# First block of the gated delta rule: the causal mask applied ahead of the exponential, and one raw buffer for z

## What is computed

```python
gcum = jnp.cumsum(g, axis=-1)
diff = gcum[..., :, None] - gcum[..., None, :]
decay = jnp.where(causal, jnp.exp(jnp.where(causal, diff, 0.0)), 0.0)
Lm = jnp.where(strict, jnp.einsum('nbhid,nbhjd->nbhij', kb, k) * decay, 0.0)   # kb = k * beta
T = lax.linalg.triangular_solve(Lm + eye, ...)                                  # inverse of Lm + eye
aqk = jnp.einsum('nbhid,nbhjd->nbhij', q, k) * decay
```

## Time and profile before

| what | value |
|---|---|
| three runs | 1980.54, 1978.75, 1978.02 us; median 1978.75 us |
| the profiled execution | 1971.89 us, its span 1970.1 us |
| mean granted clock of TensorE | 0.964 |
| first delta-rule block, from SyncE's first load to ScalarE's last output | 294.58 to 384.65 us |
| TensorE busy over the whole span | 93% |

### The profile page before, as it was taken

How to read it: one execution, slowest core, us unless ns; L and a number is a source line. 1 busy time by engine, 2 the same in 40 slices (tenths; PEclk the granted TensorE clock), 3 DMA queues, 4 the chain that set the end, 5 groups by cost and what they waited for, 6 DMA issues and landing times. The chain is left out here.

```text
span 1970.1 us, 24088 instructions
## 1 busy us (share of the span) xinstructions
PE 1833.9 (93%) x8588; PEld 1521.2 (77%) x8588; DVE 1496.0 (76%) x1118; ACT 1108.3 (56%) x891; POOL 366.4 (19%) x317
## 2 busy tenths in 40 slices
PE   6999997897999974999999999999999999999991
PEld 5888876796888873788888888888888888888870
DVE  4336567566232645899999999999999999999976
ACT  4123443243331214777777777777777777777751
POOL 0000006142000010322222213222222121221320
PEclk9999997898999986999999999999999999999995
DMA  4322225103233254799999999999999999999955
GB/s 152 107 86 86 85 86 179 29 8 122 93 130 105 73 190 172 313 382 391 366 392 380 379 393 369 386 391 370 389 376 380 395 365 390 395 365 392 377 223 233
DMA packets 124396, 516.93 MB, mean 262 GB/s; under 512 B 20772, under 2 KB 20964, under 8 KB 90244
## 3 DMA queue, kind: packets, MB, share of 16 engines
q1 hardware_dynamic: 114996, 482.30, 63.9%
q0 software_dynamic: 9360, 34.08, 4.3%
HBM read 492.19 MB, written 24.15 MB: 262 GB/s over the span
## 5 line engine op out<-in xcount | busy, mean ns | idle before, releaser
L1609 DVE TENSOR_TENSOR mlo<-mraw,mhi 128x2048 fp32r<-128x2048 f32 x384 | 908.3, 2399 | 62.3 <-ACT mhi L1605 58.4
L1605 ACT ACTIVATE mhi<-mraw 128x2048 fp32r<-128x2048 f32 x384 | 722.7, 1913 | 114.2 <-PE PM L1982 114.2
L1979 PE MATMUL PM<-mhi,xgT_hi 128*128 128x512 f32 x1024 | 404.4, 395 | 0.0
L1980 PE MATMUL PM<-mlo,xgT_hi 128*128 128x512 f32 x1024 | 401.1, 392 | 0.0
L1982 PE MATMUL PM<-mhi,xgT_lo 128*128 128x512 f32 x1024 | 276.4, 392 | 0.0
L1980 PEld LDWEIGHTS PM<-mlo,xgT_hi 128*128 128x128 f32 x1024 | 192.9, 188 | 41.7
L1982 PEld LDWEIGHTS PM<-mhi,xgT_lo 128*128 128x128 f32 x1024 | 192.3, 188 | 42.2
L1979 PEld LDWEIGHTS PM<-mhi,xgT_hi 128*128 128x128 f32 x1024 | 192.8, 188 | 41.0
L1998 PE MATMUL PM<-mhi,hT_hi 128*128 128x512 f32 x512 | 203.9, 398 | 2.6 <-DVE hT_lo L1928 2.6
L1999 PE MATMUL PM<-mlo,hT_hi 128*128 128x512 f32 x512 | 200.5, 392 | 0.0
L1817 POOL TENSOR_TENSOR glu<-glu 128x1024 f32<-128x1024 f32 x32 | 77.2, 2411 | 576.9 <-DVE glu L1923 576.9
(11 more groups left out here) (313 smaller groups left out, 2566.4 us busy)
## 6 DMA issues: line engine op xcount, KB each, us to landing
mraw<-in_w_gate_up_dram SPq DMA_DIRECT2D x256, 1024.0 KB, 8.4
mraw<-in_w_down_dram SPq DMA_DIRECT2D x128, 1024.0 KB, 9.3
raw<-in_w_in_dram SPq DMA_DIRECT2D x24, 1024.0 KB, 5.1
qkvT<-in_w_in_dram SPq DMA_DIRECT2D x8, 1024.0 KB, 5.7
mraw<-expert_rows_scratch SPq DMA_DIRECT2D x8, 1024.0 KB, 10.8
zraw<-in_w_in_dram SPq DMA_DIRECT2D x4, 1024.0 KB, 6.1
qkvT<-in_w_o_gdn_dram SPq DMA_DIRECT2D x4, 1024.0 KB, 5.0
qkvT<-in_w_o_sconv_dram SPq DMA_DIRECT2D x4, 1024.0 KB, 5.1
```

Source lines behind the costliest of these rows:

```text
L1605: nc.scalar.activation(mhi[:, split_slot(m), :], mraw[:, raw_slot(m), :], ACT.Copy).then_inc(e_h, 1)
L1609: nc.vector.tensor_tensor(mlo[:, split_slot(m), :], mraw[:, raw_slot(m), :], mhi[:, split_slot(m), :].bitcast(F32), ALU.subtract).then_inc ...
L1979: pe.matmul(gate_up_bank[:, n, :], xgT_hi[:, k, :], w_hi[:, n, :], start=False, stop=False)
L1980: pe.matmul(gate_up_bank[:, n, :], xgT_hi[:, k, :], w_lo[:, n, :], start=False, stop=False)
```

## The change

In the first block the mask is put into `aqkT` before the exponential: where a key's token is after the query's, GpSimd's `affine_select` writes -1e30, and the exponential makes that zero. The subtraction of the token's own decay becomes the bias of the exponential, which so takes eight instructions for a chunk, one for each head; `ngc`, the negated decays, is a new small copy on VectorE. The minimum with zero and the multiplication by `tri` go. The multiplication of `LT` by `aqkT` moves from GpSimd to VectorE (`decayed_gates`), ahead of each chunk's `products`. `zraw` has one slot instead of two, so each of the four z loads waits for the `z_low` before it, and they stand elsewhere in SyncE's order; on ScalarE the second `z_hi` now comes after all the exponentials. VectorE's `z_low(0,0)` comes ahead of the copy of the beta row, and `z_low(1,0)` after products(3). `U` is laid out from the first block on: GpSimd zeroes both slots at its beginning, and SyncE loads the inverses of chunks 0 and 1 at its end and waits for them there. In the second block only chunks 2 and 3 are loaded and cleared.

```diff
@@ -532,8 +533,9 @@
         LT = p2_sb("LT", [P, TT, HEADS, P])
-        by_tok = p2_sb("by_tok", [P, 13, TH])
-        gtok, btok, gc, eg, egl, ekd, ssk, rk, brk, ebk, qeps, brow, inv = (by_tok[:, n, :] for n in range(13))
+        by_tok = p2_sb("by_tok", [P, 14, TH])
+        gtok, btok, gc, eg, egl, ekd, ssk, rk, brk, ebk, qeps, brow, inv, ngc = (by_tok[:, n, :] for n in range(14))
+        U = p2_sb("U", [P, 2, HEADS, P])
         minus_half = p2_sb("minus_half", [P, TH])
@@ -583,7 +585,7 @@
         def pa_sb(name, shape, dt=F32):
-        zraw = pa_sb("zraw", [P, 2, GT, GW])
+        zraw = pa_sb("zraw", [P, GT, GW])
         zhi = pa_sb("zhi", [P, 2, GT, GW], F32R)
@@ -615,8 +618,8 @@
             def _(sp):
                 def load_z(zg, kq):
-                    wait(sp, z_l, 2 * zg + kq - 1)
-                    sp.dma_start(zraw[:, kq, :, :], Z_SOURCES[zg][:, kq * GT:(kq + 1) * GT, :]).then_inc(s_zraw[kq], 16)
+                    wait(sp, z_l, 2 * zg + kq)
+                    sp.dma_start(zraw[:], Z_SOURCES[zg][:, kq * GT:(kq + 1) * GT, :]).then_inc(s_zraw, 16)
@@ -625,7 +628,6 @@
                 load_z(0, 0)
-                load_z(0, 1)
                 sp.wait_ge(s_grow, 1)
@@ -638,31 +640,38 @@
                                  ).then_inc(s_bin[c], 16)
+                load_z(0, 1)
+                blocks_out(0)
+                blocks_out(1)
                 load_z(1, 0)
-                blocks_out(0)
-                load_z(1, 1)
-                for c in range(1, TT):
-                    blocks_out(c)
+                blocks_out(2)
+                blocks_out(3)
                 sp.wait_ge(s_nb, 16 * QB * TT)
                 sp.dma_start(W[:].rearrange("p j i -> p (j i)"), nb_d).then_inc(s_W, 16)
+                load_z(1, 1)
                 sp.wait_ge(s_solved, 1)
...
                 sp.wait_ge(s_ub, 16)
+                for c in range(2):
+                    sp.wait_ge(s_uz, c + 1)
+                    for b in range(QB):
+                        rows = slice(b * BLK, (b + 1) * BLK)
+                        sp.dma_start(U[rows, c, :, rows], blocks_of(ub_d, c)[b]).then_inc(s_uin[c], 16)
+                for c in range(2):
+                    sp.wait_ge(s_uin[c], 16 * QB)
...
             def _(pool):
...
                 nc.gpsimd.memset(minus_half[:], -0.5).then_inc(s_ones, 1)
+                for c in range(2):
+                    nc.gpsimd.memset(U[:, c], 0.0).then_inc(s_uz, 1)
                 for c in CHUNKS:
                     for g in BOTH:
-                        pool.wait_ge(s_exp, 2 * c + g + 1)
-                        nc.gpsimd.tensor_tensor(half(aqkT[:, c], g), half(aqkT[:, c], g), each(tri[:]),
-                                                ALU.mult).then_inc(s_tri, 1)
-                    for g in BOTH:
-                        pool.wait_ge(s_bin[c], 16)
-                        pool.wait_ge(s_tri, 2 * c + g + 1)
-                        nc.gpsimd.tensor_tensor(half(LT[:, c], g), half(LT[:, c], g), half(aqkT[:, c], g),
-                                                ALU.mult).then_inc(s_decL, 1)
+                        pool.wait_ge(s_gin[c], 16)
+                        nc.gpsimd.affine_select(out=half(aqkT[:, c], g), in_=half(aqkT[:, c], g), compare_op=ALU.is_ge,
+                                                fill=FAR_BELOW, base=0, pattern=[[0, HS], [1, P]], channel_multiplier=-1
+                                                ).then_inc(s_tri, 1)
                 pool.wait_ge(s_redk, 2 * TT + 1)
@@ -680,13 +689,16 @@
                 def exps(c):
                     for g in BOTH:
-                        act.wait_ge(s_diff, HEADS * c + HS * g + HS)
-                        nc.scalar.activation(half(aqkT[:, c], g), half(aqkT[:, c], g), ACT.Exp).then_inc(s_exp, 1)
+                        act.wait_ge(s_tri, 2 * c + g + 1)
+                        for h in range(HS * g, HS * (g + 1)):
+                            n = c * HEADS + h
+                            ins = nc.scalar.activation(aqkT[:, c, h, :], aqkT[:, c, h, :], ACT.Exp, bias=ngc[:, n:n + 1])
+                        ins.then_inc(s_exp, 1)
                 def z_hi(zg, kq):
-                    act.wait_ge(s_zraw[kq], 16 * (zg + 1))
+                    act.wait_ge(s_zraw, 16 * (2 * zg + kq + 1))
                     wait(act, z_grp if kq else z_used, zg)
-                    nc.scalar.activation(zhi[:, kq, :, :], zraw[:, kq, :, :], ACT.Copy).then_inc(z_h, 1)
+                    nc.scalar.activation(zhi[:, kq, :, :], zraw[:], ACT.Copy).then_inc(z_h, 1)
@@ -703,15 +715,13 @@
                 z_hi(0, 0)
-                act.wait_ge(s_gc, 3)
+                act.wait_ge(s_gc, 4)
                 nc.scalar.activation(eg, gc, ACT.Exp).then_inc(s_small, 1)
...
                 nc.scalar.activation(ekd, ekd, ACT.Exp).then_inc(s_small, 1)
-                exps(0)
-                exps(1)
+                for c in CHUNKS:
+                    exps(c)
                 z_hi(0, 1)
-                exps(2)
-                exps(3)
                 z_hi(1, 0)
@@ -732,16 +742,16 @@
-                def differences(c):
-                    dve.wait_ge(s_gin[c], 16)
-                    for h in range(HEADS):
-                        row = aqkT[:, c, h, :]
-                        nc.vector.tensor_scalar(row, row, gc[:, c * HEADS + h:c * HEADS + h + 1], 0.0, ALU.subtract,
-                                                ALU.min).then_inc(s_diff, 1)
+                def decayed_gates(c):
+                    dve.wait_ge(s_bin[c], 16)
+                    for g in BOTH:
+                        dve.wait_ge(s_exp, 2 * c + g + 1)
+                        nc.vector.tensor_tensor(half(LT[:, c], g), half(LT[:, c], g), half(aqkT[:, c], g),
+                                                ALU.mult).then_inc(s_decL, 1)
                 def z_low(zg, kq):
                     dve.wait_ge(z_h, 2 * zg + kq + 1)
-                    nc.vector.tensor_tensor(zlo[:, kq, :, :], zraw[:, kq, :, :], zhi[:, kq, :, :].bitcast(F32),
+                    nc.vector.tensor_tensor(zlo[:, kq, :, :], zraw[:], zhi[:, kq, :, :].bitcast(F32),
                                             ALU.subtract).then_inc(z_l, 1)
@@ -762,6 +772,7 @@
                 nc.vector.tensor_copy(gc, PB[:, 7, 0, 0:TH]).then_inc(s_gc, 1)
+                nc.vector.tensor_scalar(ngc, PB[:, 7, 0, 0:TH], -1.0, None, ALU.mult).then_inc(s_gc, 1)
                 nc.vector.tensor_copy(egl, PB[:, 7, 0, TH:2 * TH]).then_inc(s_gc, 1)
@@ -775,20 +786,17 @@
                                                op1=ALU.mult).then_inc(s_brow, 1)
-                dve.wait_ge(s_gc, 3)
-                differences(0)
+                z_low(0, 0)
                 dve.wait_ge(s_browT, 1)
                 nc.vector.tensor_copy(row_sb[:, 1, :], PB[0:TH, 0, 0, :]).then_inc(s_brs, 1)
-                differences(1)
-                z_low(0, 0)
-                differences(2)
-                differences(3)
-                products(0)
+                for c in range(2):
+                    decayed_gates(c)
+                    products(c)
                 z_low(0, 1)
-                products(1)
-                products(2)
+                for c in range(2, TT):
+                    decayed_gates(c)
+                    products(c)
                 z_low(1, 0)
-                products(3)
                 dve.wait_ge(s_brow, 1)
@@ -926,7 +932,7 @@
             def _(sp):
-                for c in CHUNKS:
+                for c in range(2, TT):
                     sp.wait_ge(s_uz, c + 1)
@@ -952,13 +958,10 @@
                 def clear(c):
-                    if c >= 2:
-                        pool.wait_ge(s_vn, 2 * (c - 2) + 2)
+                    pool.wait_ge(s_vn, 2 * (c - 2) + 2)
                     nc.gpsimd.memset(U[:, c % 2], 0.0).then_inc(s_uz, 1)
-                clear(0)
                 masks(0)
-                clear(1)
                 decayed_keys(0)
```

More of the change, by code:

```diff
@@ L527, in hybrid_block @@
         TH = TT * HEADS
+        FAR_BELOW = -1e30
         p2 = ExitStack()
@@ L603, in hybrid_block @@
         s_rk, s_brk = mixer_sem("s_k_norms"), mixer_sem("s_beta_norms")
-        s_diff, s_exp, s_small = mixer_sem("s_decay_diff"), mixer_sem("s_decay_exp"), mixer_sem("s_small_exps")
+        s_exp, s_small = mixer_sem("s_decay_exp"), mixer_sem("s_small_exps")
+        s_uz, s_uin = mixer_sem("s_U_zeroed"), [mixer_sem(f"s_U_loaded{n}") for n in range(2)]
         s_tri, s_decL = mixer_sem("s_decay_causal"), mixer_sem("s_decay_beta")
         s_GA, s_AT, s_LT = mixer_sem("s_qk_kk_products"), mixer_sem("s_aqkT"), mixer_sem("s_LT")
-        s_zraw = [mixer_sem(f"s_z_weights_loaded{k}") for k in range(2)]
+        s_zraw = mixer_sem("s_z_weights_loaded")
         z_h, z_l, z_used, z_grp, z_bank = (mixer_sem("s_z_hi"), mixer_sem("s_z_lo"), mixer_sem("s_z_chunk_used"),
@@ L845, in z @@
                             if zg == 0:
-                                pe.wait_ge(s_gc, 3)
```

(3 more changed lines are left out.)

## The result

In the first comparison the changed kernel ran in 1965.51 us (median of 4, 1964.76 to 1966.33) against 1978.38 us before (median of 4): a ratio of 0.9942, with a 95% interval of 0.9931 to 0.9954. That is **12.9 us faster; 6.9 were forecast**, and the time lies under the range (1967.5 to 1977.0). On other chips the kernel before had 1977.2 (21 runs), 1975.0 (9) and 1977.0 us (9). On the second of these the changed kernel was timed again, at 1964.06 us (5 runs): 10.9 us faster. What the change is worth lies near 11 to 13 us.

What follows compares the result with a forecast made beforehand. TensorE's turn of `U` was taken as the bound, delayed by a 7.45 us hole before products(1). Following the chain, it moved from 389.65 to 382.8 us: 1978.75 - 6.9 = 1971.8 us, range 1967.5 to 1977.0.

Steps and rivals of the forecast that it cites:

- The mechanism: First block: VectorE's differences take 0.91 us each beside GpSimd's multiplications because the two take turns, delaying products(1).
- the hole: TensorE's idleness of 7.45 us before products(1) at 328.14 us, ended by VectorE's line 754.
- TensorE without a hole: After products(0), TensorE runs on without idling; products(3) begin at 334.9 us instead of 342.27.
- the sum: The forecast's step-by-step chain through the first block to the turn of `U`, at 382.8 instead of 389.65: -6.9 us.
- The solve and the way to it: Last `LT` ready at 339.2 us, `W` at 345.6, 0.9 us of waiting at a `z_low`, inverses out at 371.0.
- The loads of `U` close the block: End of first block: eight loads take 5.5 us, land at 379.2, 2.0 us after z; block opens at 379.5.
- the 16 turns: Second block, ahead of the turn of `U`: 3.3 us, the middle of 2.62 and 3.94.
- drain one by one: Rival, 6 in 100, slower: block's end waits for eight landings of `U` in a row; 1988.3 us at 2.75 apiece.
- the selects: GpSimd's eight selects of 128x512: 1.1 us each; in the lock rival (13 in 100) over 2.25 us, 1977.0 at 2.9.
- Beta row, later by 1.8 us: First block: `z_low(0,0)` ahead of the copy, which starts at 310.1 us instead of 308.30.
- The sum applied to the median: The 6.9 us gain taken from the 1978.75 us median, though the profiled execution was 1971.89: 1971.8 us.
- the deep case: Rival, 12 in 100: eight loads of `U` as fast as four and turns at 2.62 us; -9.3 us, 1969.4.

Runs made afterwards that it cites:

- pool_held: Kernel before plus one wait: GpSimd begins its masks and gates only when all 32 differences on VectorE are done; 1965.94 us, ratio 0.9952.
- u_late: Changed kernel with the loads of `U` of chunks 0 and 1 back in the second block; 1962.82 us, ratio 0.9931.
- the third profile: The kernel before, unchanged, profiled a third time; 1977.91 us (1 run).
- copy_first: Changed kernel with the copy of the beta row put back ahead of `z_low(0,0)`; 1961.22 us, ratio 0.9922.
- the three common profiles: Second, third and fourth profiles of the unchanged kernel before; times 1976.85 (11 runs), 1977.91 and 1977.42 us (1 run each).
- after_again: The changed kernel, unchanged, timed and profiled a second time; 1964.06 us (5 runs), ratio 0.9947 against the kernel before.

## Why the prediction was wrong, step by step

- **The mechanism** (VectorE and GpSimd exclude each other, this makes the hole, the hole is the gain): right, shown by pool_held.
- **TensorE without a hole**: right. From the copy of the beta row to the start of the last product into `LT` the sum had 338.5 - 310.1 = 28.4 us; the profile has 335.94 - 307.49 = 28.45.
- **The solve and the way to it**: right. 25.85 us from `W` to the issue of the inverses, forecast 25.4; `z_low` waited 1.42 us for ScalarE, forecast 0.9.
- **The loads of `U` close the block**: right, 5.9 us with the opening for 5.8, and the 16 turns took 3.44 us for 3.3. No rival happened: the loads did not drain one by one, the selects stayed under 2.3 us, and neither they nor the exponentials (387 ns) held anything up.
- **"Beta row, later by 1.8 us": absent from the measured pair, by luck.** The sum had the copy 15.5 us after the entry; it comes 13.7 us after it in both first profiles. The two executions did not have the same front. The windows of the first profile of before, and then of the changed kernel:

```profile
298.00:302.00 4.00, 4.00 (x19) 3.29 (x18) 1.96 (x7) 3.36 (x8) 0.00 (x0) 0.50 0.95 357
```

```profile
298.00:302.00 4.00, 2.43 (x20) 1.91 (x19) 3.15 (x10) 4.00 (x10) 0.00 (x0) 1.00 0.20 73
```

  At the granted clock of 0.50 the turns of k take longer, and the beta row is formed 11.5 us after the entry; at 1.00 it is formed 10.0 us after it. u_late has the changed kernel's first block, with a slow front (row formed at 11.5 us). The timelines of TensorE's entry and of VectorE's copy in it:

```profile
291.66 1.09 PE L814 MATMUL PB<-ident,ab 128*128 128x128 f32 x4 [4.04 <-PEq L187]
```

```profile
306.83 0.27 DVE L784 COPY row_sb<-PB 32x128 f32<-32x128 f32 x1
```

  There the copy comes 15.2 us after the entry, against 13.7 and 13.6 in the two profiles of before with a slow front: 1.5 us later, nearly the 1.8 of the sum. With a fast front the charge is nothing (13.7 and 13.6 against 13.5 and 13.9), because in the kernel before the copy stands behind differences(0), which then wait for the decay broadcasts (1.77 us in the third profile, between 304.3 and 306.1): the change replaces one wait by another. The sum took one front for both kernels. Against a copy that waits for nothing the charge is 3 us, which is what copy_first measures.
- **The sum applied to the median: the step that failed most.** I saw that the profiled execution was 6.9 us under the median and treated that as an offset common to both kernels. It was not. That execution had a short hole and a short rest. Against the three common profiles the block is 11.2 us shorter (98.3 in the mean to 87.1 in the mean of two), against the first one 8.1 and 10.2. Of the 4.3 us between the forecast 6.85 and those 11.2, 2.1 are this base and 1.8 the beta row; the remaining 0.4 are less than the 2.1 us by which the two profiles of the changed kernel differ. The rest behind the block is 1574.7 to 1573.7 in the mean, 1.0 us, within what executions of one kernel differ by.
- So the range was too narrow at its lower end: the gap between profile and median was itself a warning that the hole's length varies, and the deep case should have reached to 11 or 12 us.

Not tried: why the hole's length, and the granted clock at the block's entry, vary between executions. The alternation of the two engines starts from when the decay rows land and when GpSimd gets its first mask, and both differ among the profiles; that this sets the hole's length is argued, not shown.

## What to carry to other kernels

When two engines take turns, look for the cheapest way to keep them apart before rewriting the work: here one wait gave more than eight tenths of the gain. An early load with a wait on it at the end of a stage can cost more than the late load it replaces; issue it and leave the wait to the consumer (here that opened the next block 1.4 us earlier). And when a profiled execution lies outside the timed runs, profile again before adding a difference to the median, because a stall that varies is exactly what such an execution may lack. Compare the front of the two profiles too: here 1.5 us of clock at the entry hid a cost of the same size.

## What the runs showed of the hardware that was not expected

- GpSimd's power of 128x32 (line 677 after) reads SBUF and by the record, which is rough for GpSimd, ran from 310.97 for 5478 ns. VectorE's first two gates, with two SBUF inputs, began at 313.13 us in the middle of it and took 1.29 us together, their normal length; so did those of after_again and u_late. So the exclusion, which the Trainium skill ("SBUF — State Buffer", SBUF's two separate sides) describes as held for the whole instruction, did not hold for this one; elementwise products and selects did exclude VectorE's. In pool_held a `z_low` of VectorE was under way when the power began, and there the power's record is 7.54 us, 2.06 longer; it ends 5.3 us after that `z_low`, as if it had waited to start. The row of the power, by its line, and in the timeline of GpSimd in pool_held:

```profile
L677 POOL TENSOR_TENSOR by_tok<-by_tok,minus_half x1: 5478/5478/5478, 311.0 to 311.0; 128x32 f32<-128x32 f32 x1
```

```profile
337.03 7.54 POOL L669 TENSOR_TENSOR by_tok<-by_tok,minus_half 128x32 f32<-128x32 f32 x1
```

- VectorE's products with one operand in PSUM and one in SBUF kept 0.67 to 0.69 us in pool_held too, where GpSimd multiplies beside them, so that form did not meet the exclusion.
- Exponentials of 128x128 with a bias by partition took 387 ns each by the record, but 32 of them 9.45 us, 0.30 us apiece: the records overlap, and the pitch is what an order of work costs.
